# Two chunks of the out projection set between the pieces of the retention

## The chip, the cores and the metric

The kernel runs on one core of a Trainium2 chip. The time is the device time of one launch in microseconds (us); lower is better. Five engines work at once, each through its own list of instructions, and wait for each other on semaphores: TensorE (PE in the rows; PEld is its loading of weights), VectorE (DVE), ScalarE (ACT), GpSimd (POOL) and SyncE (SP), which here issues the loads from HBM.

## The reference

The program is a stack for 512 tokens of width 1024. First come two hybrid layers, and only they are touched. Each computes, from a normed x,

```
aq, ak, av, ag, rq, rk, rv, rg = split(rms_norm(x) @ w_in)
ya = chunked_rel_attention(aq, ak, av, rel_bias)     # 8 heads of 64
yr = chunkwise_retention(rq, rk, rv, cos, sin)       # 4 heads of 128
y  = concat([ya * silu(ag), yr * silu(rg)])          # 1024 columns
x  = x + y @ w_out                                   # the out projection
```

A retention head multiplies its scores q.k by a decay mask, multiplies that with v, and divides each token's result by its root mean square. Behind the two layers come four feed-forward blocks, a convolution block and a stick-breaking attention, which the change leaves alone. Everything is float32.

## The kernel before, in words

**Products in three parts.** A projection isn't multiplied in plain float32. Each operand is split into a rounded high part and the low part that is left, and `product` (L1483 to 1487) issues three matmuls of 512 columns: high by high, high by low, low by high. Retention scores, retention values, sums and rows of numbers are multiplied in plain float32.

**Chunks.** Weights come in chunks of 128x2048 into two slots of `raw`. SP loads a chunk when the low part of the one before it in its slot is made (`lo_ready`). ScalarE makes the high part, `w_hi` (`high_part`, L633), once TensorE is done with the slot's former chunk (`chunk_done`); GpSimd makes the low part, `w_lo`, by a subtraction (`low_pair`, L517). The convolution's stage lets VectorE do that by a function `low` (L1314). An out projection has four chunks; a chunk makes two tiles of 128 output columns, and takes eight steps over k (the eight tiles of y), each of two products, so six matmuls. Here such a step is called a piece: piece (c, k) is step k of chunk c. Chunk c goes to two PSUM banks, 0 and 1 for even c, 2 and 3 for odd c.

**Attention loop.** In each hybrid layer, TensorE's list mixes the attention (16 units, four to each pair of heads) with the products of the retention's q, k, gate and v. When a pair is through, VectorE multiplies its values with its gate (`att_gated`, L1183).

**Retention.** Then come two halves of two heads each (loop at L1730 on TensorE, L1235 on VectorE, L808 on ScalarE). Each head has four score matmuls (L1741), each multiplied by the decay on VectorE (L1241), and four value matmuls (L1748). After that: squares on ScalarE (L812), sums of them by TensorE (L1492), square roots (ScalarE, L815), reciprocals and a multiplication with the gate (VectorE, L1251 and L1253), rows of the reciprocals by TensorE (L1499), and on VectorE the scaling, the high part and the low part of y (L1259 to L1261; L1262 signals). In the slack of each half VectorE also splits two of the attention's four tiles of y (L1246, L1247). The second half's first scores wait for the first half's y (`y_split`). Scores lie in banks 0 and 1, values in 4 and 5, sums in 2 and 3, rows in 6 and 7.

**Out projection.** `out_layer` (L1606) runs all four chunks after the retention. Chunk 0 is rounded and split during the attention. The high part of chunk 1 stands on ScalarE's list behind the whole retention. After each chunk VectorE adds its tiles to x (L1017), splits them for the next layer (L935, L936) and adds up their squares (L944), which ScalarE makes (L695); in the second layer it also multiplies by the final gain (L1024). On ScalarE's list the high part of chunk c + 2 stands behind the squares of chunk c - 1, and GpSimd's low part behind that. The order is written out by hand; there is no planner.

Of the kernel before, what the change touches and what calls it, by code (L numbers as in the profile page):

```python
# [157 lines left out]
def build(nc, x_t, positions, vecs_d, bias_d, decay_d, w_feat, w_tok, w_out, w_up, w_down, w_pw1, w_pw2,  # L158
# [64 lines left out]
    ret_masked = [region("ret_masked0", 0, [P, ST, SEQ]), region("ret_masked1", 2048, [P, ST, SEQ])]  # L223
    y_hi = region("y_hi", 4096, [P, KD, SEQ], f32r)
# [97 lines left out]
    ret_rows = semaphore("ret_rows")  # L322
    angles_ready = semaphore("angles_ready")
# [185 lines left out]
    def _(pool):  # L509
        link = Tally(pool_link)  # L510

        def low_pair(name, i):
            w = width(name)
            for s in range(2):

                pool.wait_ge(hi_ready, first[name] + 2 * i + s + 1)
                nc.gpsimd.tensor_tensor(w_lo[:, s, 0:w], raw[:, s, 0:w], w_hi[:, s, 0:w].bitcast(f32),  # L517
                                        ALU.subtract).then_inc(lo_ready, 1)
# [104 lines left out]
    def _(act):  # L623
# [137 lines left out]
        for l in range(DEPTH):  # L761
# [44 lines left out]
            values_by_token(f"ret_v{l}", ret_v, 0)(0, 1)  # L806

            for i in range(RET_HEADS // 2):  # L808
                h0 = RET_HEADS * l + 2 * i
                for s in range(2):  # L810
                    act.wait_ge(ret_values, h0 + s + 1)
                    nc.scalar.activation(tmp[:, s, :], ps[:, 4 + s, :], ACT.Square).then_inc(ret_squares, 1)  # L812
                for s in range(2):
                    act.wait_ge(ret_sums, h0 + s + 1)
                    nc.scalar.activation(ret_root[:, ST * s:ST * (s + 1)], ps[:, 2 + s, 0:ST],  # L815
                                         ACT.Sqrt, scale=1.0 / RET_DIM, bias=eps_rms).then_inc(ret_roots, 1)
            layer(f"out{l}", squares_of_two(["att_in1", "final_gain"][l]))
# [106 lines left out]
    def _(dve):  # L924
# [78 lines left out]

        def update_two(name, norm, bias_name=None, split_gain=None, gain=None):
# [3 lines left out]
            for c in range(4):  # L1008
                dve.wait_ge(chunk_done, first[name] + c + 1)
                for t in range(2):  # L1010
# [7 lines left out]
                    ins.then_inc(x_updated, 1)  # L1018
                for t in range(2):
# [95 lines left out]
        for l in range(DEPTH):  # L1115
# [68 lines left out]

            def ret_rotated(n):
# [34 lines left out]
            for i in range(ATT_UNITS + 3):  # L1220
# [4 lines left out]
                if i < ATT_UNITS:  # L1225
                    att_biased(i)
                for n in range(12):
# [4 lines left out]
            dve.wait_ge(gate_out, gates_before[name] + 4)  # L1232

            for i in range(RET_HEADS // 2):
                h0 = RET_HEADS * l + 2 * i  # L1235
                dve.wait_ge(decay_loaded[i], 16 * (l + 1))
                for s in range(2):
                    dve.wait_ge(ret_values, h0)
                    for kt in range(ST):
                        dve.wait_ge(ret_scores, ST * (h0 + s) + kt + 1)  # L1240
                        nc.vector.tensor_tensor(ret_masked[s][:, kt, P * kt:SEQ], ps[:, kt % 2, 0:SEQ - P * kt],  # L1241
                                                decay[:, 2 * i + s, 0:SEQ - P * kt], ALU.mult)\
                            .then_inc(masked_ready, 1)
                for s in range(2):
                    j = 2 * i + s
                    then(nc.vector.tensor_copy(y_hi[:, j, :], gates[:, j, :]))  # L1246
                    nc.vector.tensor_tensor(y_lo[:, j, :], gates[:, j, :], y_hi[:, j, :].bitcast(f32),  # L1247
                                            ALU.subtract).then_inc(y_split, 1)
                for s in range(2):
# [3 lines left out]
                    then(nc.vector.tensor_tensor(tmp[:, 2 + s, :], ps[:, 4 + s, :], gates[:, 4 + 2 * i + s, :],  # L1253
                                                 ALU.mult))
                for s in range(2):
# [3 lines left out]
                    then(nc.vector.tensor_tensor(y, y, ps[:, 6 + s, :], ALU.mult))  # L1259
# [48 lines left out]

        def low(name, c):

            if (name, c) == ("pw1", 2):
                dve.wait_ge(lo_ready, first["pw1"] + 2)
            dve.wait_ge(hi_ready, first[name] + c + 1)
            nc.vector.tensor_tensor(w_lo[:, c % 2, :], raw[:, c % 2, :], w_hi[:, c % 2, :].bitcast(f32),  # L1314
                                    ALU.subtract).then_inc(lo_ready, 1)
# [166 lines left out]
    def _(pe):  # L1482
# [123 lines left out]
        def out_layer(name, next_norm, source=(x_hi, x_lo)):  # L1606

            for c in range(4):
# [36 lines left out]
        for l in range(DEPTH):  # L1645
# [85 lines left out]
            pe.wait_ge(v_ready, v_no[f"ret_v{l}"] + 1)  # L1731
            pe.wait_ge(heads_out, ATT_PAIRS * (l + 1))
# [267 lines left out]
```

## Time and profile before

| | |
|---|---|
| median of 3 runs | 2609.86 us (2606.67 to 2611.96) |
| the profiled execution's own time | 2606.49 us |
| its span, first to last instruction | 2604.8 us |
| mean granted TensorE clock | 0.989 |
| TensorE busy | 2527.6 us, 97% |
| VectorE, GpSimd, ScalarE busy | 1063.0, 987.2, 714.7 us |
| first layer's retention | about 236 to 271 us of the span |
| second layer's retention | about 539 to 575 us |

A row of a timeline has the start in us from the span's start, the duration in us, the engine, the line, the operation, what it writes and reads, and how many instructions are merged into it; in brackets stands how long the engine was idle before it and which instruction ended that wait. Ends of matmuls are modelled, so the distance from one start to the next tells more than the duration.

### The profile page before, as it was taken

The numbers are of one execution on the slowest core, as the hardware profiler recorded it, in microseconds if no ns is written. First come the engines' busy times: TensorE is split into PE (matmuls) and PEld (weight loads), VectorE is DVE, ScalarE is ACT, GpSimd is POOL, SyncE is SP. The second block draws the span as 40 slices with busy tenths as digits, with TensorE's granted clock in tenths as the row PEclk, the third lists the DMA queues.
The fourth block names the chain that finished last, engine by engine and source line by source line (L and its number), as shares of the span: only waits on it lengthen the run. The fifth ranks groups of instructions, "written<-read, shape, count | busy, mean of one in ns | idle before, by whom it ended". The sixth has DMA issues, their size and how long they took to land.

```text
span 2604.8 us, 30359 instructions
## 1 busy us (share of the span) xinstructions
PE 2527.6 (97%) x11718; PEld 1998.9 (77%) x11718; DVE 1063.0 (41%) x1587; ACT 714.7 (27%) x930; POOL 987.2 (38%) x321
## 2 busy tenths in 40 slices
PE   9998999989999999989999999999999989999998
PEld 7765787667888888658888888888888666888886
DVE  5463715548422315965223110422311666522301
ACT  3333223323222222242222222222222453222221
POOL 3321343213444433124444444444444553444442
PEclk9999999999999999999999999999999989999999
DMA  4321132212222232512222333322224001222222
GB/s 154 113 81 49 65 113 89 81 41 82 90 97 96 81 100 101 139 45 96 97 97 82 100 109 118 133 95 96 85 92 171 33 17 34 96 97 97 82 100 76
DMA packets 42322, 235.84 MB, mean 91 GB/s; under 512 B 5504, under 2 KB 5504, under 8 KB 21888
## 3 DMA queue, kind: packets, MB, share of 16 engines
q1 hardware_dynamic: 42096, 232.60, 25.9%
q10 hardware_dynamic: 144, 2.10, 0.2%
q8 instruction: 57, 0.93, 0.2%
q14 instruction: 25, 0.20, 0.0%
HBM read 222.86 MB, written 6.29 MB: 88 GB/s over the span
## 4 chain that ended last, share of the span: by engine, by line
PE 90%; DVE 6%; ACT 2%; issue 1%; SPq 0%; DMA 0%; POOL 0%; DVEq 0%; ACTq 0%
PE ps L1485 27%; PE ps L1487 27%; PE ps L1486 27%; PE ps L1873 2%; PE ps L1779 1%; PE ps L1741 1%; PE ps L1712 1%; PE ps L1499 1%; PE ps L1748 1%; PE ps L1859 1%; PE ps L1691 1%; PE ps L1886 1%; PE ps L1700 1%; DVE small L1168 1%; DVE score L1162 0%
## 5 line engine op out<-in xcount | busy, mean ns | idle before, releaser
L517 POOL TENSOR_TENSOR w_lo<-raw,w_hi 128x2048 fp32r<-128x2048 f32 (+1 forms) x206 | 874.3, 4244 | 1422.0 <-ACT w_hi L633 1396.9
L1485 PE MATMUL ps<-x_hi,w_hi 128*128 128x512 f32 x2048 | 810.3, 396 | 9.4 <-DVE sb_q L1401 2.8
L1487 PE MATMUL ps<-x_hi,w_lo 128*128 128x512 f32 x2048 | 799.6, 390 | 0.0
L1486 PE MATMUL ps<-x_lo,w_hi 128*128 128x512 f32 x2048 | 798.6, 390 | 0.0
L1485 PEld LDWEIGHTS ps<-x_hi,w_hi 128*128 128x128 f32 x2048 | 385.1, 188 | 109.2 <-issue 24.2
L633 ACT ACTIVATE w_hi<-raw 128x2048 fp32r<-128x2048 f32 (+1 forms) x216 | 377.6, 1748 | 328.6 <-PE ps L1487 325.1
L1487 PEld LDWEIGHTS ps<-x_hi,w_lo 128*128 128x128 f32 x2048 | 384.9, 188 | 81.0
L1486 PEld LDWEIGHTS ps<-x_lo,w_hi 128*128 128x128 f32 x2048 | 385.5, 188 | 75.9
L1046 DVE TENSOR_TENSOR tmp<-ps,rms_b 128x512 f32<-128x512 f32 x88 | 60.9, 692 | 589.2 <-PE ps L1487 578.7
L1487 PE MATMUL ps<-hid_hi,w_lo 128*128 128x512 f32 x704 | 278.4, 395 | 0.0
L1485 PE MATMUL ps<-hid_hi,w_hi 128*128 128x512 f32 x704 | 278.3, 395 | 0.0
L1486 PE MATMUL ps<-hid_lo,w_hi 128*128 128x512 f32 x704 | 278.3, 395 | 0.0
L722 ACT ACTIVATE tmp<-tmp 128x512 f32<-128x512 f32 x88 | 55.7, 633 | 699.5 <-DVE tmp L1046 699.4
L1071 DVE SCALAR_TENSOR_TENSOR x<-ps,x 128x512 f32 x32 | 22.1, 692 | 389.2 <-PE ps L1487 389.2
L1485 PEld LDWEIGHTS ps<-hid_hi,w_hi 128*128 128x128 f32 x704 | 132.2, 188 | 32.2
L1486 PEld LDWEIGHTS ps<-hid_lo,w_hi 128*128 128x128 f32 x704 | 132.2, 188 | 32.1
L1487 PEld LDWEIGHTS ps<-hid_hi,w_lo 128*128 128x128 f32 x704 | 132.1, 188 | 32.0
L695 ACT ACTIVATE tmp<-x 128x512 f32<-128x512 f32 (+1 forms) x64 | 39.8, 633 | 338.4 <-DVE x L1071 237.5
L944 DVE TENSOR_TENSOR sq_sum<-sq_sum,tmp 128x512 f32<-128x512 f32 x72 | 106.3, 1476 | 9.8 <-ACT tmp L695 7.3
L604 POOL TENSOR_TENSOR soft_lo<-tmp,soft_hi 128x128 fp32r<-128x128 f32 (+3 forms) x64 | 62.2, 972 | 71.4 <-DVE soft_hi L1440 71.4
L1054 DVE TENSOR_TENSOR hid_lo<-tmp,hid_hi 128x512 f32 (+1 forms) x88 | 84.9, 964 | 10.6
L1485 PE MATMUL ps<-w_hi,x_hi 128*128 128x512 f32 x192 | 77.5, 404 | 2.8 <-issue 2.8
(211 smaller groups left out, 2500.1 us busy)
## 6 DMA issues: line engine op xcount, KB each, us to landing
raw<-in_w_up SPq DMA_DIRECT2D x88, 1024.0 KB, 4.9
raw<-in_w_down SPq DMA_DIRECT2D x64, 704.0 KB, 4.1
raw<-in_w_feat SPq DMA_DIRECT2D x23, 1024.0 KB, 4.9
raw<-in_w_pw SPq DMA_DIRECT2D x12, 1024.0 KB, 5.0
raw<-in_w_tok SPq DMA_DIRECT2D x8, 1024.0 KB, 4.9
raw<-in_w_out SPq DMA_DIRECT2D x8, 1024.0 KB, 4.9
shifted<-conv_in SPq DMA_DIRECT2D x80, 67.5 KB, 2.1
bias<-in_bias_t SPq DMA_DIRECT2D x8, 512.0 KB, 6.1
```

The costliest lines, as they stand in the source:

```text
L517: nc.gpsimd.tensor_tensor(w_lo[:, s, 0:w], raw[:, s, 0:w], w_hi[:, s, 0:w].bitcast(f32), ALU.subtract).then_inc(lo_ready, 1)
L604: nc.gpsimd.tensor_tensor(soft_lo[:, soft_span(u)], tmp[:, u % 6, 0:SPAN[u % 8 // 2]], soft_hi[:, soft_span(u)].bitcast(f32), ALU.subtract ...
L633: nc.scalar.activation(w_hi[:, s, 0:w], raw[:, s, 0:w], ACT.Copy).then_inc(hi_ready, 1)
L695: nc.scalar.activation(tmp[:, slot, :], x[:, j, :], ACT.Square).then_inc(squares_ready, 1)
L722: nc.scalar.activation(tmp[:, s, :], tmp[:, s, :], func, bias=bias_col).then_inc(gate_out, 1)
L944: nc.vector.tensor_tensor(sq_sum[:, :], sq_sum[:, :], tmp[:, slot, :], ALU.add)\
L1046: nc.vector.tensor_tensor(tmp[:, s, :], ps[:, 2 * s, :], rms_b[:, :], ALU.mult)\
L1054: nc.vector.tensor_tensor(hid_lo[:, j, :], tmp[:, 2 + s, :], hid_hi[:, j, :].bitcast(f32), ALU.subtract).then_inc(hidden_ready, 1)
L1485: nc.tensor.matmul(out, hi, src_hi, start=start, stop=False, skip_group_check=True)
L1486: nc.tensor.matmul(out, hi, src_lo, start=False, stop=False, skip_group_check=True)
L1487: return nc.tensor.matmul(out, lo, src_hi, start=False, stop=stop, skip_group_check=True)
L1873: ins = nc.tensor.matmul(ps[:, Z_BANK[u % 6], P * (r - later):SPAN[r]], weights[:, :], part[:, at], start=False, stop=later == r and part ...
```

## The change

In both hybrid layers:

- TensorE's list has sixteen pieces of chunks 0 and 1 moved into and behind the retention: six in the first half, (0,0) to (0,3), (1,0), (1,1), and three in the second, (0,4), (0,5), (1,2); seven more follow the retention. `out_layer` then runs chunks 2 and 3 alone.
- To free banks 0 to 3 for them, the retention's scores, sums and rows share banks 4 and 5, and its values take 6 and 7. A new semaphore, `ret_scaled`, guards the reuse of 4 and 5 by the second half's scores; their wait for `y_split` is gone.
- VectorE splits each attention tile right after its gating, in the attention loop (`att_split`); `y_hi` and `ret_masked` change places in SBUF.
- ScalarE makes the high part of chunk 1 ahead of the retention's squares.
- VectorE makes the low part of chunk 2 between the two steps of `update_two` for chunk 0; GpSimd makes those of chunks 0, 1 and 3.

```diff
-            low_parts(f"out{l}")
+            low_pair(f"out{l}", 0)
+            pool.wait_ge(lo_ready, first[f"out{l}"] + 3)
+            low_part(f"out{l}", 1, 1)
...
             values_by_token(f"ret_v{l}", ret_v, 0)(0, 1)
+            high_part(f"out{l}", 0, 1)
...
-            layer(f"out{l}", squares_of_two(["att_in1", "final_gain"][l]))
+            layer(f"out{l}", squares_of_two(["att_in1", "final_gain"][l]), second_rounded=True)
...
+                if c == 0 and name.startswith("out"):
+                    low(name, 2)
                 for t in range(2):
                     j = 2 * c + t
                     dve.wait_ge(x_updated, updates[norm] + j + 1)
...
+            def att_split(pair):
+                dve.wait_ge(heads_out, ATT_PAIRS * l + pair + 1)
+                then(nc.vector.tensor_copy(y_hi[:, pair, :], gates[:, pair, :]))
+                nc.vector.tensor_tensor(y_lo[:, pair, :], gates[:, pair, :], y_hi[:, pair, :].bitcast(f32),
+                                        ALU.subtract).then_inc(y_split, 1)
...
-                    then(nc.vector.tensor_tensor(y, y, ps[:, 6 + s, :], ALU.mult))
+                    nc.vector.tensor_tensor(y, y, ps[:, 4 + s, :], ALU.mult).then_inc(ret_scaled, 1)
+                    dve.wait_ge(ret_scaled, h0 + s + 1)
...
+            def out_products(c, k):
+                if k == 0:
+                    pe.wait_ge(lo_ready, first[out] + c + 1)
+                    pe.wait_ge(v_ready, v_no[f"ret_v{l}"] + 1)
+                pe.wait_ge(y_split, KD * y_no[out] + k + 1)
+                for t in range(2):
+                    at = (KD * t + k) * P
+                    ins = product(ps[:, 2 * c + t, :], w_hi[:, c, at:at + P], w_lo[:, c, at:at + P],
+                                  y_hi[:, k, :], y_lo[:, k, :], k == 0, k == KD - 1)
+                if k == KD - 1:
+                    ins.then_inc(chunk_done, 1)
...
-                pe.wait_ge(y_split, KD * y_no[f"out{l}"] + 4 * i)
...
+                    elif i:
+                        pe.wait_ge(ret_scaled, h0 - 1 + kt)
...
+                scores(0, 0)
+                scores(0, 1)
+                if i == 0:
+                    out_products(0, 0)
+                scores(0, 2)
+                scores(0, 3)
+                if i == 0:
+                    out_products(0, 1)
                 scores(1, 0)
                 scores(1, 1)
+                if i == 0:
+                    pe.wait_ge(v_ready, v_no[f"ret_v{l}"] + 1)
                 values(0)
                 scores(1, 2)
                 scores(1, 3)
+                if i == 0:
+                    out_products(0, 2)
+                    pe.wait_ge(heads_out, ATT_PAIRS * (l + 1))
                 values(1)
...
+                out_products(0, 3 if i == 0 else 4)
+                sums()
+                if i == 0:
+                    out_products(1, 0)
+                else:
+                    out_products(0, 5)
+                rows()
+                out_products(1, 1 if i == 0 else 2)
+            for c, k in ((0, 6), (1, 3), (0, 7), (1, 4), (1, 5), (1, 6), (1, 7)):
+                out_products(c, k)
+            out_layer(out, ["att_in1", "final_gain"][l], (y_hi, y_lo), start=2)
```

## Rows read from the trace of the kernel before

**Rows 1.** The page: the chain that ended last, by engine.
```profile
PE 90%; DVE 6%; ACT 2%; issue 1%; SPq 0%; DMA 0%; POOL 0%; DVEq 0%; ACTq 0%
```
**Rows 2.** Windows: stretch, length, busy time by engine, granted clock, DMA share, GB/s.
```profile
235.55:271.23 35.68, 29.61 (x130) 20.41 (x129) 19.23 (x42) 7.44 (x13) 0.00 (x0) 0.90 0.00 0
250.40:253.60 3.20, 3.20 (x16) 3.18 (x16) 2.40 (x6) 0.00 (x0) 0.00 (x0) 0.52 0.00 0
539.34:575.02 35.68, 29.61 (x130) 20.44 (x129) 19.23 (x42) 7.44 (x13) 0.00 (x0) 0.90 0.00 0
```
**Rows 3.** Waits of PE, 235 to 350 us: total, times, longest.
```profile
PE ps L1741 <- DVE small L1262: 2.4, 1, 2.4
```
**Rows 4.** Timeline of PE around the first layer's retention.
```profile
234.50 1.09 PE L1712 MATMUL ps<-tmp,v_tok 128*64 128x128 f32 x16
237.08 1.77 PE L1741 MATMUL ps<-ret_qk 128*128 128x512 f32 x4 [1.49 <-ACT ret_v L732]
...
241.91 2.32 PE L1748 MATMUL ps<-ret_masked,ret_v 128*128 128x512 f32 x8
244.07 0.82 PE L1741 MATMUL ps<-ret_qk 128*128 128x256 f32 x4
245.38 2.42 PE L1748 MATMUL ps<-ret_masked,ret_v 128*128 128x512 f32 x8 [0.49 <-DVE ret_masked L1241]
...
267.68 1.90 PE L1492 MATMUL ps<-ones,tmp 128*128 128x1 f32 x16
269.44 2.03 PE L1499 MATMUL ps<-ident,small 128*128 128x128 f32 x16
271.23 0.48 PE L1485 MATMUL ps<-y_hi,w_hi 128*128 128x512 f32 x1
271.55 0.39 PE L1486 MATMUL ps<-y_lo,w_hi 128*128 128x512 f32 x1
```
**Rows 5.** Timeline of DVE in the same stretch.
```profile
235.64 0.69 DVE L1183 TENSOR_TENSOR gates<-ps,gates 128x512 f32<-128x512 f32 x1 [10.54 <-PE ps L1712]
...
245.24 0.42 DVE L1246 CAST y_hi<-gates 128x512 fp32r<-128x512 f32 x1
...
246.30 0.42 DVE L1246 CAST y_hi<-gates 128x512 fp32r<-128x512 f32 x1
...
252.28 0.69 DVE L1259 TENSOR_TENSOR tmp<-tmp,ps 128x512 f32<-128x512 f32 x1 [0.69 <-PE ps L1499]
...
254.20 0.68 DVE L1259 TENSOR_TENSOR tmp<-tmp,ps 128x512 f32<-128x512 f32 x1
```
**Rows 6.** Timelines of DVE and POOL at the attention loop's step 6.
```profile
147.71 0.68 DVE L1194 TENSOR_TENSOR tmp<-ps,rope_rms 128x512 f32<-128x512 f32 x1
...
149.00 4.55 POOL L517 TENSOR_TENSOR w_lo<-raw,w_hi 128x2048 fp32r<-128x2048 f32 x1 [12.49 <-ACT w_hi L633]
```
**Rows 7.** Line L1314: count, shortest, median and longest in ns.
```profile
L1314 DVE TENSOR_TENSOR w_lo<-raw,w_hi x9: 2278/2284/3384, 1010.8 to 2025.8; 128x2048 fp32r<-128x2048 f32 x9
```
**Rows 8.** Timelines of ACT, DVE and POOL behind the retention, first layer.
```profile
282.77 1.92 ACT L633 ACTIVATE w_hi<-raw 128x2048 fp32r<-128x2048 f32 x1 [11.08 <-PE ps L1487]
...
295.11 0.48 DVE L935 TENSOR_SCALAR x_hi<-x,vecs 128x512 fp32r<-128x512 f32 x1
...
296.90 0.48 DVE L935 TENSOR_SCALAR x_hi<-x,vecs 128x512 fp32r<-128x512 f32 x1
```
**Rows 9.** The same, second layer.
```profile
593.65 0.48 DVE L1024 TENSOR_SCALAR x<-x,vecs 128x512 f32<-128x512 f32 x1
...
595.96 0.48 DVE L1024 TENSOR_SCALAR x<-x,vecs 128x512 f32<-128x512 f32 x1
...
597.70 1.29 DVE L1017 TENSOR_TENSOR x<-ps,x 128x512 f32<-128x512 f32 x2
...
601.54 5.09 POOL L517 TENSOR_TENSOR w_lo<-raw,w_hi 128x2048 fp32r<-128x2048 f32 x1 [8.36 <-ACT w_hi L633]
...
608.90 1.29 DVE L1017 TENSOR_TENSOR x<-ps,x 128x512 f32<-128x512 f32 x2 [0.68 <-PE ps L1487]
```

More of the change, by code:

```diff
@@ L322, in build @@
     ret_rows = semaphore("ret_rows")
+    ret_scaled = semaphore("ret_scaled")
     angles_ready = semaphore("angles_ready")
@@ L1002, in wait_rms, with low @@
             dve.wait_ge(rms_ready, sum_no[norm] + 1)
+        def low(name, c):
+            if name != "pw2" and c == 2:
+                dve.wait_ge(lo_ready, first[name] + 2)
+            dve.wait_ge(hi_ready, first[name] + c + 1)
+            nc.vector.tensor_tensor(w_lo[:, c % 2, :], raw[:, c % 2, :], w_hi[:, c % 2, :].bitcast(f32),
+                                    ALU.subtract).then_inc(lo_ready, 1)
         def update_two(name, norm, bias_name=None, split_gain=None, gain=None):
@@ L1226, in _ @@
                     att_biased(i)
+                if i >= 3 and (i - 3) % ST == ST - 1:
+                    att_split((i - 3) // ST)
                 for n in range(12):
@@ L1240, in _ @@
                         dve.wait_ge(ret_scores, ST * (h0 + s) + kt + 1)
-                        nc.vector.tensor_tensor(ret_masked[s][:, kt, P * kt:SEQ], ps[:, kt % 2, 0:SEQ - P * kt],
+                        nc.vector.tensor_tensor(ret_masked[s][:, kt, P * kt:SEQ], ps[:, 4 + kt % 2, 0:SEQ - P * kt],
                                                 decay[:, 2 * i + s, 0:SEQ - P * kt], ALU.mult)\
                             .then_inc(masked_ready, 1)
[L1244 to L1248, printed above, removed]
+                dve.wait_ge(gate_out, gates_before[name] + 4)
                 for s in range(2):
@@ L1604, in values_layer, with out_layer @@
                 ins.then_inc(chunk_done, 1)
-        def out_layer(name, next_norm, source=(x_hi, x_lo)):
-            for c in range(4):
+        def out_layer(name, next_norm, source=(x_hi, x_lo), start=0):
+            for c in range(start, 4):
                 if c < 2:
@@ L1751, in values, with sums, rows @@
                     ins.then_inc(ret_values, 1)
-                for kt in range(ST):
-                    scores(0, kt)
+                def sums():
+                    for s in range(2):
+                        pe.wait_ge(ret_squares, h0 + s + 1)
+                        sum_over_features(tmp[:, s, :], 4 + s, 0, ret_sums)
+                def rows():
+                    for s in range(2):
+                        pe.wait_ge(ret_invs, h0 + s + 1)
+                        rows_of(ret_inv[:, ST * s:ST * (s + 1)], 4 + s, ret_rows)
+                scores(0, 0)
[6 more added lines that the diff above has]
+                    out_products(0, 1)
                 scores(1, 0)
                 scores(1, 1)
+                if i == 0:
+                    pe.wait_ge(v_ready, v_no[f"ret_v{l}"] + 1)
                 values(0)
@@ L1759, in _ @@
                 scores(1, 3)
+                if i == 0:
+                    out_products(0, 2)
+                    pe.wait_ge(heads_out, ATT_PAIRS * (l + 1))
                 values(1)
-                for s in range(2):
-                    pe.wait_ge(ret_squares, h0 + s + 1)
-                    sum_over_features(tmp[:, s, :], 2 + s, 0, ret_sums)
-                for s in range(2):
-                    pe.wait_ge(ret_invs, h0 + s + 1)
-                    rows_of(ret_inv[:, ST * s:ST * (s + 1)], 6 + s, ret_rows)
-            out_layer(f"out{l}", ["att_in1", "final_gain"][l], (y_hi, y_lo))
+                out_products(0, 3 if i == 0 else 4)
[9 more added lines that the diff above has]
+            out_layer(out, ["att_in1", "final_gain"][l], (y_hi, y_lo), start=2)
         layer("up0", "up0", "up0")
```

35 lines of the change are left out of this document (15 added, 20 removed).

## The prediction

> **What bounds the kernel now.** I read the page first: the chain that ended last is 90% TensorE [rows 1], so a change pays only where TensorE stands still, runs at its lower clock, or does less. Then I looked for such places with windows over the span, and the retention is one: in each layer TensorE is busy 29.61 us of 35.68 at a mean granted clock of 0.90 [rows 2]. Both layers show the same figures, so one is worked out and the other taken from it. In a stretch of 3.2 us the clock is 0.52, so at 1.2 GHz, half of full speed, nearly throughout; it stands just behind TensorE's waits for squares, roots and reciprocals, and a like drop follows the next wait. The list of waits names the longest, 2.4 us before the second half's scores, for VectorE's last y [rows 3]. The timeline gives TensorE's own work at full clock, from start to start: values of a head 2.16 us (241.91 to 244.07), scores of a head about as much, since they have the same columns, sums of a half 1.76, rows 1.79 [rows 4]. Four heads and two halves: 4 x 4.3 + 2 x 3.55 = 24.3 us. So 35.7 - 24.3 = 11.4 us a layer are waits or slow clock.
>
> **The change, part by part.** The two chunks' own work stays. A chunk takes 11.2 us (VectorE's additions at 597.70 and 608.90 [rows 9]), a piece 1.40. What can be won is the 11.4 us. Before, retention and two chunks end at 271.23 + 22.4 + 0.1 = 293.7 us.
>
> Step 1, changes of number format. The first product behind float32 matmuls takes 0.32 us to the next instead of 0.23 (271.23 to 271.55 [rows 4], against 1.40 / 6). I take as much for the way back, so a piece set alone among them costs about 0.19. There are eight such pieces more than before: 1.5 us a layer. From below the cost is nothing where it falls into a wait.
>
> Step 2, the first half. The scores no longer wait 1.49 us for ScalarE's value copies [rows 4] and start at 235.55, when the attention's last matmuls (234.50, 1.09) are through. The last attention tile is gated at 235.64, its split takes 1.06 more (245.24 to 246.30 [rows 5]) plus 0.1, so VectorE masks from 237.6; TensorE meanwhile does two scores and piece (0,0), to 238.7. From there each mask has a piece before it is needed. Walking the list: (0,1) ends at 241.0, values of the first head at 244.6, (0,2) at 246.9, values of the second at 249.0, (0,3) at 250.6, sums at 252.4, (1,0) at 254.0, rows at 255.8, (1,1) at 257.4, with no wait at all. ScalarE's load of the root's table now lies under (0,3).
>
> Step 3, chunk 1 ready. ScalarE makes its high part behind the value copies, which end at 237.0 (the first score's wait [rows 4]), so until 239.0, GpSimd its low part to about 243.7. (1,0) wants it at 252.4: hidden by 8 us. What VectorE does in those 4.6 us is masking out of PSUM; if it had to wait for GpSimd, three masks would be some 4 us late, and the cover of three pieces gone. I take nothing, with 4 us a layer as the far bound. SP's load of chunk 3 is released some 33 us earlier and meets no other load.
>
> Step 4, the second half. VectorE's last y of the first half comes behind the rows: scaling, high and low part take 1.92 us a head (252.28 to 254.20 [rows 5]); that ends at 259.0. TensorE is at the third score by 258.9 and waits for the first mask, 0.9 us; here only two scores cover it. Then 0.45 before the next head, and 0.65 before the second values, as there the row shows 0.49 now [rows 4]. So 2.0 us of waits a layer stay. `ret_scaled` itself comes at 257.8, when TensorE wants it at 258.2. (0,4), (0,5) and (1,2) cover squares, roots and the last y; (0,6) starts at 276.4, its y is there at 276.2. Seven pieces: chunk 0 ends at 280.6, chunk 1 at 286.1. Won: 293.7 - 286.1 = 7.5 us a layer. As a check, 11.4 - 1.5 - 2.0 = 7.9; I keep the walk.
>
> Step 5, the attention loop. Three `att_split`s of 1.1 us go to VectorE's list there. TensorE waits for none of what follows at steps 10 and 14, as VectorE's timeline has idle time soon behind both places. At step 6 the split falls between the reduction's end at 147.7 and GpSimd's low part at 149.0 [rows 6]; it would end at 148.85. If it came late, its subtraction would wait for GpSimd until 153.6, and the rotation behind it would end 3 us late: up to 2.3 us a layer. I take nothing.
>
> Step 6, behind the retention. Count from the end of chunk 0. Chunk 1 now ends 5.6 us later, not 11.2. ScalarE rounds chunk 2 from 0.2 to 2.1 (1.92 us [rows 8]). VectorE's low part takes 2.28 us [rows 7]: ready at 4.6, wanted at 5.6. GpSimd's 4.6 us [rows 6] would end at 6.8 and cost 1.2. But VectorE's part delays chunk 1's addition: the two tiles of chunk 0 come after it, 1.79 us each in the first layer (295.11 to 296.90 [rows 8]) and 2.31 in the second (593.65 to 595.96 [rows 9]), so that addition starts at 8.1 and 9.2 instead of 5.8. The high part of chunk 3 stands behind its squares, and GpSimd starts 3.84 us after the addition (597.70 to 601.54) and takes up to 5.09 [rows 9]: the low part is ready at 16.9 and 18.2. TensorE wants it when chunk 2 ends, at 5.6 + 11.2 = 16.8. That costs 0.1 in the first layer and 1.4 in the second. In the second layer VectorE then meets chunk 2's end 2.9 us late, makes part of it good in its 0.68 us of slack a chunk [rows 9], and is still 0.6 late for chunk 3; its chain of gain, squares and norm ends TensorE's waits at the start of the next block, so 0.6 is lost again. Second layer: 2.0.
>
> The Trainium skill speaks against the move to VectorE: its page Perfetto Trace Analysis (Optimizing Scalar/DVE Operations) says that VectorE and GpSimd share a read port of SBUF, so that shifting work between them might not help. By that rule the low part would be worth no more on VectorE, and each layer would lose some 1.2 us here and 2.3 more in the delay of the addition. The rows of L1314 bear it out only in their longest (3384 ns); the median of 2284 was against an idle GpSimd, and GpSimd is idle here too, so I go by the median.
>
> **Sum.** 7.5 - 0.1 + 7.5 - 2.0 = 12.9 us. The profiled execution took 2606.49 us, so its like would take 2593.6. The median of the runs is 3.4 above it, and 2609.86 - 12.9 gives 2597. I state 2596, between the two and nearer to the median.
>
> **The rivals.** First, it wins more: the format changes vanish in waits and GpSimd's low part comes in time, 1.5 + 1.5 + 2.1 us, perhaps 1 or 2 of the second half's waits: 18 to 20 us, about 2591. For it: these are my least sure terms. Against: each has its row.
>
> Second, the clock still falls in the second half. There 0.9, 0.45 and 0.65 us of waits come within 7 us, and sums of one column go ahead. Before, a drop of 3.2 us cost 1.6 us [rows 2]. If two such come back in each layer, 6.4 us go and 2603 is left. Against it: before, the second half with its wait of 0.49 and sums and rows on end kept full clock.
>
> Third, it doesn't do what it says: the pieces run, but TensorE waits as long elsewhere, for a mask behind GpSimd (step 3, 4 us a layer) or a late split (step 5, 2.3): 2607 to 2609. Against it: of VectorE's reads from PSUM beside GpSimd's low parts none that I saw was held; but no mask was among them.
>
> Fourth, slower: the clock doesn't just dip but stays at 1.2 GHz through the mixed stretch. A microsecond there loses 0.5, so it decides from 13 us a layer on (6.5 of gain). With 20 us a layer 10 are lost, and the time is 2609.86 - 13 + 20 = 2617. For it: the second half has many format changes and waits. Against it: the drop shown is 3.2 us, and the attention loops, mixed in just this way, lie in a span whose mean clock is 0.989.
>
> **How the numbers follow.** Forecast 50%, more won 17%, clock 19%, not what it says 8%, slower 6%. A measurement can tell about 0.2%, or 5.2 us, from no change. Faster by that is the forecast, the first rival and most of the second: 0.85. Within it are the third and a rest of the second: 0.09. Slower: 0.06. The range goes from 2589 (first rival, with a median as low as the profiled run) to 2604 (second rival with a step 5 that costs).
>
> **What would show it.** The window from the first retention score to the end of chunk 1 should be near 50.6 us at a clock of 1.00, where it was 58.1. The waits of 2.4 us for L1262 and of 1.49 for the value copies should be gone; in their place a wait of about 0.9 on the first mask of the second half. `low`'s line should take 2.28 us in both out projections. Ahead of chunk 3's first product, TensorE should wait about 1.4 us for GpSimd in the second layer and hardly at all in the first. If the clock row is under 0.95 the second rival holds; if masks exceed 0.69 us, the third does.

## The result, and the profile after

| | before | changed |
|---|---|---|
| median | 2609.86 us (5 runs, 2606.34 to 2614.79) | 2594.03 us (5 runs, 2591.82 to 2595.17) |
| ratio, 95% interval | | 0.9942 (0.9931 to 0.9953) |
| the profiled execution, its span | 2606.49, 2604.8 us | 2591.82, 2590.1 us |
| mean granted TensorE clock | 0.989 | 0.991 |

The changed kernel is faster by 15.8 us. 12.9 was forecast, as 2596 us in a range of 2589 to 2604.

First a view that misleads. The page's chain, by engine, after the change:

```profile
PE 71%; DVE 4%; ACT 1%; issue 1%; SPq 0%; POOL 0%; DMA 0%; DVEq 0%; ACTq 0%
```

Beside [rows 1] TensorE seems to have lost 19% of the span to nobody. The shares here add up to 77%, those of before to 99%: the chain wasn't followed to the start of the span. So the two aren't comparable, and TensorE's busy time is the same 97% of the span in both. What can be compared is a stretch between two instructions that both kernels have. I use two, in each layer. A goes from the start of the attention's last value matmuls to the first product of chunk 2: retention and both moved chunks, whatever their order. B goes on to the first scaling by the norm that follows (the first feed-forward block's, in the second layer), so that it holds what chunks 2 and 3 pay.

Windows of before, A in either layer; the columns are as in [rows 2]:

```profile
234.50:293.71 59.21, 53.14 (x242) 39.37 (x241) 36.43 (x58) 11.80 (x17) 9.61 (x2) 0.94 0.09 33
538.29:597.50 59.21, 53.14 (x241) 39.40 (x241) 36.78 (x60) 11.79 (x17) 9.26 (x2) 0.94 0.10 36
```

Windows after: A and B of the first layer, A and B of the second, and a stretch of the second layer's attention:

```profile
233.48:284.18 50.70, 48.96 (x242) 36.85 (x241) 24.24 (x49) 11.91 (x17) 4.55 (x1) 1.00 0.06 21
284.18:321.74 37.56, 37.56 (x171) 30.46 (x170) 30.12 (x30) 10.02 (x12) 14.58 (x3) 1.00 0.33 113
530.35:581.03 50.68, 48.94 (x242) 36.84 (x241) 24.25 (x49) 11.90 (x17) 4.55 (x1) 1.00 0.06 21
581.03:632.52 51.49, 48.77 (x225) 39.34 (x223) 43.94 (x50) 17.54 (x23) 19.73 (x4) 1.00 0.26 89
514.00:520.00 6.00, 3.88 (x18) 2.78 (x18) 3.82 (x3) 2.47 (x7) 4.53 (x1) 0.72 0.09 17
```

TensorE issues as many matmuls in A as before (242) and is done in 50.7 us instead of 59.2, at a clock of 1.00 instead of 0.94. So A gives 8.5 us a layer. B was 37.38 and 49.76 us before: it gives back 0.2 in the first layer and 1.7 in the second. Together 8.51 + 8.53 - 0.18 - 1.73 = 15.1 us. The medians are 15.8 us apart, with an interval of 12 to 18 us by the ratio's.

The two profiled executions differ by 14.7 us of span. The first layer has 8.3 of them, the second 6.8. Another 1.0 us was won before the first retention: the attention's last matmuls start at 233.48 here and at 234.50 before. It arises in the first 10 us, where no code differs: the first product starts at 9.10 here and at 10.04 before, and between 9.2 and 10.2 in the kernels of the experiments. And 1.4 us were lost in the second layer's attention: the last row above shows a clock of 0.72 there, which before did not have.

The waits of TensorE, after, from 235 to 350 us and then from 530 to 655 us (total, times, longest):

```profile
PE ps L1765 <- DVE ret_masked L1263: 1.2, 2, 1.0
PE ps L1773 <- DVE ret_masked L1263: 0.5, 1, 0.5
```

```profile
PE ps L1496 <- DVE tmp L1064: 2.1, 1, 2.1
PE ps L1765 <- DVE ret_masked L1263: 1.2, 2, 1.0
PE ps L1496 <- POOL w_lo L516: 1.2, 1, 1.2
PE ps L1510 <- DVE small L969: 0.5, 1, 0.5
PE ps L1773 <- DVE ret_masked L1263: 0.5, 1, 0.5
```

The wait of [rows 3] is gone, and so is the one for the value copies. What is left of A's waits is 1.73 us in either layer, all in the second half and all for masks. New in the second layer are 1.2 us for GpSimd ahead of chunk 3 (L1496), and the 0.5 at the next block's rows (L1510) were 0.2 before; the 2.1 us for L1064 belong to the feed-forward block and stood before as well.

TensorE's timeline after, around the points that the prediction named:

```profile
233.48 1.09 PE L1723 MATMUL ps<-tmp,v_tok 128*64 128x128 f32 x16
234.50 1.77 PE L1765 MATMUL ps<-ret_qk 128*128 128x512 f32 x4
236.11 0.47 PE L1496 MATMUL ps<-y_hi,w_hi 128*128 128x512 f32 x1
236.41 0.39 PE L1497 MATMUL ps<-y_lo,w_hi 128*128 128x512 f32 x1
...
237.34 0.40 PE L1498 MATMUL ps<-y_hi,w_lo 128*128 128x512 f32 x1
237.57 0.81 PE L1765 MATMUL ps<-ret_qk 128*128 128x256 f32 x4
...
255.26 1.67 PE L1765 MATMUL ps<-ret_qk 128*128 128x512 f32 x4
257.91 0.95 PE L1765 MATMUL ps<-ret_qk 128*128 128x256 f32 x4 [0.98 <-DVE ret_masked L1263]
259.13 1.77 PE L1765 MATMUL ps<-ret_qk 128*128 128x512 f32 x4 [0.26 <-DVE ret_masked L1263]
...
264.20 2.42 PE L1773 MATMUL ps<-ret_masked,ret_v 128*128 128x512 f32 x8 [0.49 <-DVE ret_masked L1263]
```

Against [rows 4] the scores start right behind the attention's last matmuls, and no wait stands before 257.91. From the first score (234.50) to the end of chunk 1 (284.18) it's 49.68 us; 50.6 was forecast. (The 58.1 that the prediction sets beside it counts from 235.55, where the score could have started before, and not from 237.08, where it did.)

### The profile page after: what moved, and what is told of

Read it like the earlier page. It is cut to its first block, busy times and chain, and to the rows that moved or that the text cites. A ratio compares the mean times of both kernels' runs of the same rounds, so it can differ in the third digit from the quotient of the medians.

```text
span 2590.1 us, 30349 instructions
## 1 busy us (share of the span) xinstructions
PE 2520.6 (97%) x11718; PEld 1993.3 (77%) x11718; DVE 1047.5 (40%) x1589; ACT 714.9 (28%) x930; POOL 976.8 (38%) x319
## 4 chain that ended last, share of the span: by engine, by line
PE 71%; DVE 4%; ACT 1%; issue 1%; SPq 0%; POOL 0%; DMA 0%; DVEq 0%; ACTq 0%
PE ps L1496 22%; PE ps L1498 22%; PE ps L1497 22%; PE ps L1922 2%; PE ps L1828 1%; PE ps L1908 1%; PE ps L1935 1%; DVE w_lo L1015 0%; DVE conv_out L1342 0%; PE ps L1510 0%; PE ps L1912 0%; SPq L480 0%; DVE tmp L1435 0%; DVE tmp L1342 0%; PE ps L1852 0%
## 5 line engine op out<-in xcount | busy, mean ns | idle before, releaser
L516 POOL TENSOR_TENSOR w_lo<-raw,w_hi 128x2048 fp32r<-128x2048 f32 (+1 forms) x204 | 863.9, 4235 | 1417.8 <-ACT w_hi L638 1393.7
L1496 PE MATMUL ps<-x_hi,w_hi 128*128 128x512 f32 x2048 | 810.0, 396 | 8.9 <-DVE sb_q L1412 2.8
L1496 PEld LDWEIGHTS ps<-x_hi,w_hi 128*128 128x128 f32 x2048 | 384.9, 188 | 108.5 <-issue 22.9
L1496 PE MATMUL ps<-hid_hi,w_hi 128*128 128x512 f32 x704 | 278.2, 395 | 0.0
L1496 PEld LDWEIGHTS ps<-hid_hi,w_hi 128*128 128x128 f32 x704 | 132.0, 188 | 32.2
L950 DVE TENSOR_TENSOR sq_sum<-sq_sum,tmp 128x512 f32<-128x512 f32 x72 | 97.9, 1360 | 8.6 <-ACT tmp L700 7.3
L1496 PE MATMUL ps<-w_hi,x_hi 128*128 128x512 f32 x192 | 78.0, 406 | 2.8 <-issue 2.8
```

Source lines behind the costliest of these rows:

```text
L950: nc.vector.tensor_tensor(sq_sum[:, :], sq_sum[:, :], tmp[:, slot, :], ALU.add)\
L1496: nc.tensor.matmul(out, hi, src_hi, start=start, stop=False, skip_group_check=True)
```

## The experiments

Edits are against the changed kernel unless another is named. Times stand beside the kernel before as it ran on the same chip: 2610.1 us (15 runs) for the repeat, the pieces behind, the pieces set where waits are left and the five steps; 2607.48 us (22 runs) for the other four. Ratios are to that. The expectations call the theory by the terms that step 2 to step 6 of the prediction use, corrected by the profile after.

### The changed kernel again

No edit.

> The changed kernel once more, unaltered, beside the others. Two stretches are compared in each layer: A, from the start of the attention's last value matmuls to chunk 2's first product (before: 59.2 us in both layers; changed: 50.7), and B, from there to the first scaling by the next norm (before 37.4 and 49.8; changed 37.6 and 51.5). My theory is that A holds all of the gain (8.5 us a layer) and B gives back 0.2 and 1.7. In its profile TensorE's clock fell in the second layer's attention loop (mean 0.91 from 510 to 530 us, about 1.4 us lost) behind the same 2.2 us wait that cost no clock before. If that is chance, it will be absent here or sit elsewhere, and the time lies between 2590 and 2595; if the change causes it, it comes again at the same place.

Measured: 2595.49 us (2592.40 to 2599.30), ratio 0.9946 (0.9932 to 0.9959). A is 50.68 and 50.70 us, B 37.59 and 51.48. So the stretches repeat to 0.03 us where TensorE's clock doesn't fall. The time is half a microsecond above the expected range.

Whether the fall of the clock in the second layer's attention is chance, this run doesn't settle. It came again at the same place, and the first layer has one at the matching place as well:

```profile
220.00:226.00 6.00, 5.18 (x22) 3.71 (x23) 3.83 (x3) 1.17 (x4) 3.52 (x1) 0.72 0.22 55
518.00:524.00 6.00, 6.00 (x27) 4.24 (x26) 3.19 (x2) 0.49 (x1) 2.51 (x1) 0.72 0.39 126
```

The last section counts these falls over all profiles.

### All sixteen pieces behind the retention

The banks, `ret_scaled`, the splits in the attention loop and VectorE's low part stay; only the pieces go back.

```
-                if i == 0:
-                    out_products(0, 0)
...
-                out_products(0, 3 if i == 0 else 4)
...
-                out_products(1, 1 if i == 0 else 2)
-            for c, k in ((0, 6), (1, 3), (0, 7), (1, 4), (1, 5), (1, 6), (1, 7)):
+            for c, k in ((0, 0), (0, 1), (0, 2), (0, 3), (1, 0), (1, 1), (0, 4), (0, 5), (1, 2),
+                         (0, 6), (1, 3), (0, 7), (1, 4), (1, 5), (1, 6), (1, 7)):
```

> All sixteen pieces stand behind the retention, in the same order among themselves; banks, early splits, chunk 1's early high part, ret_scaled and VectorE's low part stay. Theory (the pieces fill TensorE's waits): the waits for squares, roots and last y come back, and the clock falls again. Only the earlier start of the scores (0.9 us a layer) and of the second half (1.3) stay won, so A is about 56 to 57 us and the time 2604 to 2607. Rival (the gain comes from the waits and splits that were taken off the path, not from the filling): A stays under 53 us and the time under 2599.

Measured: 2603.86 us (2602.61 to 2606.15), ratio 0.998 (0.9971 to 0.9989). A is 55.62 and 55.61 us. Its window in the first layer:

```profile
233.75:289.37 55.62, 50.39 (x242) 37.16 (x242) 24.25 (x49) 11.79 (x17) 4.52 (x1) 1.00 0.06 19
```

and TensorE's waits in it:

```profile
PE ps L1765 <- DVE ret_masked L1263: 2.5, 4, 1.1
PE ps L1773 <- DVE ret_masked L1263: 1.1, 2, 0.6
PE ps L1510 <- DVE small L1269: 0.8, 1, 0.8
PE ps L1765 <- DVE tmp L1277: 0.8, 1, 0.8
```

The waits add up to 5.2 us, where the changed kernel keeps 1.7, and A is 4.9 us longer: the pieces do fill waits. But the listed waits are only 3.5 of the 4.9. The other 1.4 are in TensorE's busy time: the same 242 matmuls take 50.39 us here and 48.96 in the changed kernel, both at a clock of 1.00. So a wait costs more than its row says. Distances from start to start show a part of it: a head's value matmuls take 2.23 us behind a wait (243.82 to 246.05 here) and 2.07 between two pieces (245.35 to 247.42 in the changed kernel). No run divides the 1.4 us further.

A and the time came out just under what was expected (56 to 57 us and 2604 to 2607), and a part of the theory fell. I had the clock come down at these waits; the window has it at 1.00 throughout, in the first layer, and the second has the same length. So the waits that this kernel has (0.26 to 1.11 us each) brought no fall of the clock.

### The scores kept back until the value copies are through

Against the kernel of the last section, one line ahead of the retention:

```
+            pe.wait_ge(v_ready, v_no[f"ret_v{l}"] + 1)
```

> The kernel with all pieces behind, and the first retention score waits again for ScalarE's value copies. In the kernel with all pieces behind, A was 55.6 us where the kernel before has 59.2, and the granted clock was 1.00 through the retention, against what I expected: it kept waits of 0.8, 0.8 and 1.1 us. If the clock before fell because of the long wait at the retention's start (1.49 us), it falls here again, and A is 58 or more. If not, A is 56.5 (the third score comes 0.9 later) at a clock of 1.00, and what brings the clock down is the 2.4 us wait for the last y, or chance.

Measured: 2607.28 us (2604.93 to 2609.43), ratio 0.9997 (0.9988 to 1.0006). A is 56.5 us and not 58, which was the outcome expected if the wait at the start doesn't bring the clock down. Windows: A in either layer, and the part of the second in which the clock fell:

```profile
235.60:292.12 56.52, 50.46 (x242) 37.16 (x242) 24.33 (x49) 11.80 (x17) 4.52 (x1) 1.00 0.05 19
536.95:593.46 56.51, 51.57 (x241) 38.25 (x241) 24.34 (x49) 11.80 (x17) 4.52 (x1) 0.97 0.06 19
552.00:558.00 6.00, 5.20 (x21) 3.55 (x20) 5.12 (x11) 0.67 (x3) 0.00 (x0) 0.72 0.01 3
```

The line costs 0.9 us a layer. The wait that it puts back is the old one, 1.49 us for ScalarE's copies in [rows 4]; some of it takes the place of the wait for the first mask (0.88 us in the last section, 0.23 here).

This kernel waits as long in the first layer as before does: its waits there add up to 6.03 us, those of before, from 234 to 294 us, to 6.07. What still parts their A's, 59.21 and 56.52, is the clock: 0.94 there, 1.00 here. TensorE's busy time says the same, 53.14 us before and 50.46 here. So in the first layer, between these profiles, 2.7 of the 8.5 us are the clock's; before had two falls there, one of them in [rows 2]. There is one profile of before, so how often its retention has them isn't known. Whether the clock falls isn't settled by the length of the waits alone: in the second layer of this kernel it did fall (0.72), and that fall cost nothing, since TensorE's slower matmuls ran where it would have waited for VectorE anyway: its waits for masks are 1.6 us there instead of 1.9, and one of 0.8 for the scaling is gone.

The whole kernel is only 0.03% from before, though its A's are 5.4 us shorter. 1.9 of them go in B (37.61 and 51.47). The other 3.5 hardly show in the medians, and where they go isn't in these stretches. Its profiled execution has clock falls elsewhere, one of them in the first attention; windows over the whole spans add up to about 51 us with a low clock here and 48 before, so the falls that it saves in A come back in other places. What brings them there is open. Open as well is what brings them in A of before: its second fall stands behind the 2.4 us wait for the last y [rows 3], and no kernel here puts that wait back.

### Pieces set where waits are left

In the second half (0,5) stays, (0,4) goes ahead of the second head's values and (1,2) behind its first two scores.

```
-                if i == 0:
-                    out_products(0, 0)
+                out_products(0 if i == 0 else 1, 0 if i == 0 else 2)
...
+                out_products(0, 2 if i == 0 else 4)
-                out_products(0, 3 if i == 0 else 4)
+                if i == 0:
+                    out_products(0, 3)
-                out_products(1, 1 if i == 0 else 2)
-            for c, k in ((0, 6), (1, 3), (0, 7), (1, 4), (1, 5), (1, 6), (1, 7)):
+                if i == 0:
+                    out_products(1, 1)
+            for c, k in ((1, 3), (0, 6), (0, 7), (1, 4), (1, 5), (1, 6), (1, 7)):
```

> Second half: (1,2) moves between its second and third score, (0,4) ahead of its second values; behind the rows come (1,3), (0,6), (0,7), (1,4) to (1,7). Theory (every wait left in the second half, 0.98 + 0.26 + 0.49 us, is only for want of other work): they go, less 0.1 for changes of format, so A is 49.0 to 49.3 in each layer and the time about 3 us under the changed kernel's, near 2591. Rival (these waits are VectorE's own chain, so filling them only moves them): A stays at 50.5 or more, with a new wait for VectorE behind the rows.

Measured: 2591.52 us (2590.22 to 2593.93), ratio 0.993 (0.9916 to 0.9943). A is 49.25 and 49.24 us, and TensorE's waits in it are:

```profile
PE ps L1765 <- DVE ret_masked L1263: 0.3, 1, 0.3
PE ps L1496 <- DVE small L1281: 0.3, 1, 0.3
```

A came as expected (49.0 to 49.3): the three waits of the second half were real time, and two pieces moved forward take away 1.4 us a layer. What is left is 0.3 us for one mask, and new is 0.3 us for a y of the last half (L1281). The ratio's interval overlaps that of the changed kernel; the stretches tell the difference, the medians don't.

### Five steps of chunk 1 left behind chunk 0

As the last one, but (0,5) goes behind the retention and chunk 0 is finished before (1,3), so that the distance from chunk 0's end to chunk 1's is five pieces instead of four.

```
-                else:
-                    out_products(0, 5)
...
-            for c, k in ((1, 3), (0, 6), (0, 7), (1, 4), (1, 5), (1, 6), (1, 7)):
+            for c, k in ((0, 5), (0, 6), (0, 7), (1, 3), (1, 4), (1, 5), (1, 6), (1, 7)):
```

> Like the last, but (0,5) moves behind the rows and (1,3) behind (0,7), so five pieces of chunk 1 and not four run after chunk 0's end. Theory (B's loss in the second layer comes from chunk 3's low part being chained behind chunk 0's end: ready 18.1 us after it, wanted 16.8): chunk 2 ends 1.4 us later after chunk 0's end, the wait of 1.2 us for GpSimd goes, B is 50.0 or less in the second layer, and A is 0.3 to 0.4 longer than with the pieces earlier. Time 1 us under that kernel's. Rival (B's loss is VectorE's longer list, which the order of pieces doesn't change): B stays at 51.3 or more.

Measured: 2591.28 us (2585.06 to 2592.19), ratio 0.9922 (0.9908 to 0.9936). A is 49.32 us in both layers, 0.07 longer than with the pieces moved forward and not 0.3 to 0.4. B is 37.40 and 50.11: nearly B of before (37.38, 49.76), and 0.1 us above the bound of 50.0 that the theory had set, where the rival wanted 51.3. TensorE's waits from 515 to 655 us, those of L1496:

```profile
PE ps L1496 <- DVE tmp L1064: 2.1, 1, 2.1
...
PE ps L1496 <- DVE small L1281: 0.2, 1, 0.2
```

No wait for GpSimd is left. So all but 0.35 us of what the second layer's B gave back came from the order of the ends: chunk 0's early end lets VectorE's extra work run into chunk 1's.

### GpSimd makes the low part of chunk 2

```
-            pool.wait_ge(lo_ready, first[f"out{l}"] + 3)
-            low_part(f"out{l}", 1, 1)
+            low_pair(f"out{l}", 1)
...
-                if c == 0 and name.startswith("out"):
-                    low(name, 2)
```

> The changed kernel, but GpSimd makes the low part of chunk 2 again. Theory (VectorE's 2.28 us hide it, GpSimd's 4.6 to 5.0 don't): the low part ends 7.1 to 7.2 us after chunk 0, TensorE wants it after 5.6, so A grows by 1.6 to 52.3 in both layers; in the second layer VectorE's squares are held behind GpSimd, chunk 3's low part ends near 20.4 where it is wanted at 18.4, and B grows from 51.5 to about 52.1. About 3 to 4 us in all, 2598 to 2600. Rival (the two share a port, so shifting the work bought nothing): A stays at 50.7 and the time at 2595.

Measured: 2600.79 us (2596.01 to 2602.29), ratio 0.997 (0.996 to 0.9979). A is 52.45 and 52.08 us, B 37.47 and 52.30: as the theory had them, to 0.2 us. The time is 0.8 us above its range. The waits of TensorE from 560 to 655 us, then VectorE's timeline and GpSimd's in the second layer:

```profile
PE ps L1493 <- POOL w_lo L516: 3.1, 2, 1.9
```

```profile
577.62 1.29 DVE L1030 TENSOR_TENSOR x<-ps,x 128x512 f32<-128x512 f32 x2 [2.13 <-PE ps L1495]
580.10 4.60 DVE L949 TENSOR_TENSOR sq_sum<-sq_sum,tmp 128x512 f32<-128x512 f32 x1 [1.20 <-issue]
```

```profile
579.57 4.58 POOL L516 TENSOR_TENSOR w_lo<-raw,w_hi 128x2048 fp32r<-128x2048 f32 x1 [38.38 <-ACT w_hi L637]
592.48 5.03 POOL L516 TENSOR_TENSOR w_lo<-raw,w_hi 128x2048 fp32r<-128x2048 f32 x1 [8.32 <-ACT w_hi L637]
```

This is the rule of the Trainium skill put to the test that the prediction weighed (Perfetto Trace Analysis, Optimizing Scalar/DVE Operations). VectorE's part took 2.29 us in both layers of the changed kernel (below), beside an idle GpSimd. GpSimd's takes 4.58, and VectorE doesn't get those microseconds for itself: its sum of squares starts half a microsecond behind and is held for 4.60 us instead of 0.69. So VectorE loses 3.9 us to GpSimd's low part where its own would take 2.3, and TensorE waits 1.6 and 1.2 us for chunk 2 besides. By stretches the move to VectorE is worth (1.75 - 0.09) + (1.40 + 0.81) = 3.9 us. That page warns that a shift between the two might not help; here it did: VectorE alone does this subtraction in half the time, 2.29 us against 4.58.

### The high part of chunk 3 ahead of the squares

Against the kernel with the pieces moved forward, in ScalarE's list of an out projection:

```
-                if not (first_pair and second_rounded):
+                if not (first_pair and second_rounded) and not name.startswith("out"):
...
+                if first_pair and name.startswith("out"):
+                    high_part(name, 1, 1)
```

> The kernel with the earlier pieces, and on ScalarE's list the high part of chunk 3 stands ahead of chunk 1's squares, not behind them. Theory (ScalarE's order chains chunk 3's low part to VectorE's late addition): GpSimd starts 2.1 us after chunk 1's end, 7.7 after chunk 0's, ends at 12.4, long before 16.8; the wait of 1.2 us goes and B is 50.0 or less in the second layer, with A at 49.25. Rival (GpSimd's early subtraction holds VectorE's splits back by more than it gives): B stays above 51, with a wait for VectorE's splits at the next block's start.

Measured: 2590.35 us (2589.94 to 2592.51), ratio 0.9938 (0.9926 to 0.995). A is 49.24 us in both layers, B 37.39 and 51.55. The theory wanted a second B of 50.0 or less, so it fell and the rival held. VectorE's timeline and GpSimd's:

```profile
579.14 4.89 DVE L943 TENSOR_SCALAR x_hi<-x,vecs 128x512 fp32r<-128x512 f32 x1
584.07 0.75 DVE L944 SCALAR_TENSOR_TENSOR x_lo<-x,vecs,x_hi 128x512 fp32r<-128x512 f32 x1
584.73 1.28 DVE L1033 TENSOR_TENSOR x<-ps,x 128x512 f32<-128x512 f32 x2
```

```profile
579.13 4.61 POOL L516 TENSOR_TENSOR w_lo<-raw,w_hi 128x2048 fp32r<-128x2048 f32 x1 [42.60 <-ACT w_hi L638]
```

GpSimd starts earlier, and with that it meets VectorE's split, 0.01 us ahead of it. An instruction of 0.48 us takes 4.89, chunk 1's addition comes 4.4 us later than it could, and the squares and the next norm with it: TensorE no longer waits for GpSimd ahead of chunk 3, but 0.6 us for it at the next block's first product and 0.8 at that block's rows.

### Chunk 0's rounding behind the attention's last transposes

All attention clock falls that I found after the change stood behind one wait, of 2.21 us (L1711, for ScalarE's `tmp`): there ScalarE rounds chunk 0 of the out projection ahead of a unit's exponentials. This edit, against the kernel with five steps left, moves that rounding behind the unit's copies:

```
-                for c in range(2, 9):
+                for c in range(2, 8):
...
+                if step_of(2 * KD * 7) == i:
+                    high_part(f"out{l}", 0, 0)
```

> The kernel with five pieces left, and ScalarE rounds chunk 0 of the out projection behind the moves of attention unit 14, not ahead of the exponentials of unit 15. All kernels so far have a TensorE wait of 2.21 us at that place in both layers (ScalarE's 1.9 us of rounding, then VectorE's scaling held behind GpSimd's low part), and behind it the clock sometimes falls (1.4 to 1.5 us each time). Theory: the wait goes in both layers, 4.4 us, and with it the falls of the clock; 2585 to 2587. Rival (the rounding only moves the wait, to unit 15's transposes or to piece (0,0)): within 1.5 us of the kernel with five pieces left.

Measured: 2586.06 us (6 runs, 2580.20 to 2588.41), ratio 0.9915 (0.9902 to 0.9929), the lowest median of all kernels here. TensorE's waits in the first layer's attention, from 180 us on, in the changed kernel and then here:

```profile
PE ps L1711 <- ACT tmp L796: 3.5, 4, 2.2
```

```profile
PE ps L1713 <- ACT tmp L796: 1.9, 4, 0.6
```

and a window of the first layer's attention here:

```profile
206.00:232.00 26.00, 25.07 (x142) 17.92 (x141) 8.64 (x16) 10.82 (x20) 5.73 (x2) 1.00 0.33 118
```

The wait is 1.6 us shorter in each layer, not gone as the theory had it (0.6 us stay), and neither attention has a fall of the clock. A (49.32, 49.33) and B (37.40, 50.11) stay as they were: chunk 0's low part starts at 223.27 us, is made by 227.9, and is wanted 8 us later. The profiled span is 4.7 us shorter than with five steps left: 3.2 for the waits, and the rest is the sum of fewer falls of the clock and a start that took 0.8 us longer (first product at 10.20 and 9.42 us). The two ratios' intervals overlap, 0.9902 to 0.9929 and 0.9908 to 0.9936; beside the changed kernel's (0.9931 to 0.9953, and 0.9932 to 0.9959 in its repeat, each to the kernel before on its own chip) this one's stands clear, by little.

## Why the prediction was right, point by point

**What bounds it.** Right. TensorE stood or ran slow for 11.4 us of the retention; 8.5 of A came back. The experiments divide them in the first layer: 2.7 for the clock, 0.9 for scores that no longer wait for the value copies, 4.9 for pieces in the place of waits. In the second layer the same chain of kernels gives the same lengths, but there the kernel with late scores had a fall of the clock too, at no cost, so there the step of 2.7 us can't be put down to falls alone.

**Step 1, number formats.** The mis-sized term, and with it float32 matmuls priced from rows that a piece doesn't precede. The first product behind plain matmuls takes 0.30 to 0.33 us (236.11 to 236.41), as in [rows 4], but the last one before them takes 0.23 (237.34 to 237.57), as any other. The way back costs nothing, a piece costs about 0.09 and not 0.19, and eight of them some 0.7 us a layer instead of 1.5. The way back even gives something: sums take 1.70 us from start to start between two pieces (248.89 to 250.59), as do the rows, where the prediction had 1.76 and 1.79. By the walk's own marks, from the first score to the end of (1,1), the first half took 20.76 us instead of 21.85, so 1.1 less; from there on it took 0.2 more. Together that's the 0.9 us by which the walk was too long.

**Step 2, the first half.** Right: no wait of TensorE stands in it, in either layer.

**Step 3, chunk 1 ready.** Right at the near bound. VectorE's masks and GpSimd's low part, after:

```profile
236.42 1.15 DVE L1263 TENSOR_TENSOR ret_masked<-ps,decay 128x512 f32<-128x512 f32 x2
238.21 0.62 DVE L1263 TENSOR_TENSOR ret_masked<-ps,decay 128x256 f32<-128x256 f32 x2 [0.64 <-PE ps L1765]
240.76 1.16 DVE L1263 TENSOR_TENSOR ret_masked<-ps,decay 128x512 f32<-128x512 f32 x2 [1.93 <-PE ps L1765]
```

```profile
237.89 4.55 POOL L516 TENSOR_TENSOR w_lo<-raw,w_hi 128x2048 fp32r<-128x2048 f32 x1 [14.49 <-ACT w_hi L638]
```

Two masks take 1.16 us beside GpSimd and 1.15 ahead of it. They read one operand from PSUM. The Trainium skill has this rule (SBUF — State Buffer, Who interferes with whom): a VectorE instruction with at most one input in SBUF doesn't contend with GpSimd, outside VectorE's two-port modes; one with two inputs there contends with a GpSimd instruction that reads SBUF. The trace agrees on both: a sum of squares, with both inputs in SBUF, takes 4.60 us in the section on GpSimd above. The rule would have closed the 4 us bound before the run.

**Step 4, the second half.** Forecast waits 0.9, 0.45 and 0.65; measured 0.98, 0.26 and 0.49. The forecast gain is 7.5 us a layer, the measured one 8.5; 0.9 of the difference is the walk's, 0.1 its rounding. The second rival asked for falls of the clock in this half; the window has 1.00 in both layers, and so has the kernel whose waits in A add up to 5.2 us.

**Step 5, the attention loop.** Right that it costs nothing at step 6, by 0.15 us. The split's subtraction ends at 147.87 and GpSimd starts at 148.02. A split pushed behind that start, to price the 2.3 us bound, wasn't tried.

**Step 6, behind the retention.** VectorE's timeline in the second layer, and GpSimd's:

```profile
575.73 1.29 DVE L1031 TENSOR_TENSOR x<-ps,x 128x512 f32<-128x512 f32 x2 [2.13 <-PE ps L1498]
577.71 2.29 DVE L1015 TENSOR_TENSOR w_lo<-raw,w_hi 128x2048 fp32r<-128x2048 f32 x1 [0.69 <-ACT w_hi L638]
...
584.54 1.28 DVE L1031 TENSOR_TENSOR x<-ps,x 128x512 f32<-128x512 f32 x2
```

```profile
588.43 4.99 POOL L516 TENSOR_TENSOR w_lo<-raw,w_hi 128x2048 fp32r<-128x2048 f32 x1 [49.12 <-ACT w_hi L638]
```

The chain runs as written: addition of chunk 1 at 584.5, GpSimd 3.9 us behind it, its low part late for chunk 3. Forecast 1.4 + 0.6 us, measured 1.18 and a wait at the next block's rows that grew from 0.21 to 0.54; B grew by 1.73. The median of [rows 7] was the right price for the low part, and not its longest.

**The sum.** Forecast 12.9 us; by the stretches 15.1. The 2.2 us between are the walk (0.9 and 0.1 a layer, so 2.0) and B, which gave back 1.9 us instead of 2.1. The 0.7 us from there to the 15.8 lie within the medians' interval. "It wins more" names two of the same terms, but needs 18 us. That the median came within 2 us of the stated 2596 has some luck in it: the sum has no term for the clock outside these stretches, and the two profiles of the changed kernel have about 38 and 44 us at low clock, before about 48 (all without the last 12 us of the span).

**A rival that was priced wrong.** The third rival says 2607 to 2609 for step 3's 4 us a layer or step 5's 2.3. By its own terms step 3 alone takes 8 us and gives about 2604, step 5 alone about 2601; only both together reach 2609. Neither happened.

## What to carry to other kernels

Compare two kernels between instructions that both have. Such a stretch repeated here to 0.03 us, while medians of five runs left some 0.2% open, and it parted kernels 1.4 us a layer apart that the medians could not. When work is set into an engine's waits, price what becomes early as well: chunk 0's earlier end cost 1.7 us until one piece more was left behind it. A wait that is filled gives back more than its row says: here 3.5 us of listed waits and 1.4 of busy time. And when a helper engine is let start earlier, look at which instruction of its neighbour it will now meet: the same subtraction on GpSimd cost nothing beside masks from PSUM and 4.4 us beside one split.

## What the runs showed of the hardware that I had not expected

- **Behind one and the same wait the clock falls in some executions and not in others.** The 2.21 us wait in the attention stands in nine of the ten profiles, twice in each. Behind 7 of these 18, TensorE ran at half clock for about 3.4 us, which costs about 1.7 when it is busy. The same kernel had one such fall in one profile (0.72 from 514 to 520 us) and two in another. With the wait cut to 0.6 us, neither of two slots had one. Before has none in its one profile, the changed kernel three in two; whether the change makes them likelier isn't shown. Other waits are steadier: behind the 1.8 us wait earlier in each attention none of the ten profiles has a fall, and behind the 2.09 us wait ahead of the second layer's next block all ten have one. So the length of the last wait alone doesn't decide it. Why one execution has a fall and the next hasn't is open. The changed kernel behind the wait of 2.09 us:

```profile
634.00:640.00 6.00, 6.00 (x20) 4.75 (x21) 5.05 (x9) 2.87 (x3) 0.24 (x1) 0.72 0.03 11
```

- **Waits alone don't make a fall either.** In the kernel with all pieces behind, eight waits of up to 1.1 us within 24 us brought none in either layer; with the one of 1.49 us back in front, one of two retentions had a fall, where before had two in each.
- **A format change costs on one side only**: 0.30 to 0.33 us instead of 0.23 for the first product behind plain float32 matmuls, nothing on the way back.
- **GpSimd holds VectorE's scaling with one input too**, where input and output lie in SBUF: 4.89 us for a split of 0.48 that began 0.01 us behind GpSimd, held until GpSimd's end. The changed kernel has the like: the multiplication by the final gain (L1040, at 588.90), 0.47 us behind GpSimd, takes 4.81 us instead of 0.48. Masks out of PSUM were not held. The same page and section of the Trainium skill names the tensor_scalar among the instructions that can contend with GpSimd, in VectorE's two-port modes, and says that the one issued first blocks the other; the durations agree, though no view here shows the mode.
